# Delta rule per pair of heads: the next pair's triangular inputs, the products on the old state, and the wait for the state stores

## The chip, the cores and the metric

The kernel runs on one core of one Trainium2 chip. The metric is the device time of one execution in microseconds, the median of several runs. The engines of the core are TensorE (PE in the profile, with its weight loads as PEld), VectorE (DVE), ScalarE (ACT), GpSimd (POOL) and SyncE (SP), which here only issues transfers and waits.

## What is computed

One inference step of two decoder layers for a prompt group (1 sequence of 512 tokens) and a sample group (8 sequences of 8 tokens, each with a state from before). The change touches only the gated delta rule of the second layer: 8 heads of width 128, in chunks. Cut to what matters:

```python
def gated_delta(q, k, v, g, beta, s0, chunk):
    gc = jnp.cumsum(rs(g), axis=2)
    kb, vb = k * beta[..., None], v * beta[..., None]
    decay = exp(where(incl, gc_i - gc_j, -inf))
    amat = where(strict, (kb @ k.T) * decay, 0)
    tmat = triangular_solve(amat + eye, eye)          # lower, unit diagonal
    u = tmat @ vb
    w = tmat @ (kb * exp(gc))
    qk = where(incl, (q @ k.T) * decay, 0)
    qg = q * exp(gc)
    kdec = k * exp(gc_last - gc)
    def step(s, inp):                                  # over the chunks
        v_new = u_c - w_c @ s
        o = qg_c @ s + qk_c @ v_new
        s = s * exp(gc_last) + kdec_c.T @ v_new
        return s, o
```

The kernel takes chunks of 128 tokens for the prompt (4 tiles) and puts the 64 sample tokens into a fifth tile. The states after the last chunk are outputs: one of 128x128 per head for the prompt, eight per head for the samples.

## The kernel before

All matrices are fp32. `gdn` works in two halves of 4 heads. A half is a row of stages: `project_conv` (input projection and convolution), `gdn_l2norm`, two calls of `gdn_pair` with two heads each, then `gdn_norm`, which starts the output. A stage (`stage`, L90) gives each engine one program. It ends when every engine's program has ended: semaphores are cleared and all engines meet at a barrier, so nothing of the next stage starts before. Two stages are thus joined by whatever engine ends last, SP included.

Within `gdn_pair` each engine has its instructions in a fixed order, first for head a = 0, then for head a = 1, and waits on counters of the others (`PE[...]`, `AC[...]`, `DV[...]`, `PO[...]` name the steps). A tile called `[P, 640]` holds the five tiles of one head. The parts of a pair are:

- **Opening.** POOL builds two inputs per head, `UG` (upper triangle times the gate, L2810) and `IB` (identity times beta, L2811). PE sums each over the partitions with a matrix of ones (`R`, `BR`, L2921 and L2922). DVE and ACT make the decay matrix from `R` (L2867, L2868, L2828) and multiply it with `BR` and with k.k (L2872, L2875) to give `LT`, and with k.q to give `QKD` (L2878). DVE then masks `LT` (L2880), subtracts it from the identity to give the first `TT` (L2881), and makes `kbg`, `kdec` (L2884, L2885) from the turned k and `vb` (L2887) from the turned v, which lie in PSUM; the last of these is the step "tok". PE turns `TT` after "tok" (L2931).
- **Inverse.** Six rounds, k = 1 to 6. POOL masks `LT` for the round (`AL`, L2818), PE makes three products (L2926), ACT and DVE take them out of PSUM (L2838, L2893, L2896).
- **Chunks.** Four steps over the prompt's tiles with the state `S` of 128x128 (L2977 to L2988, L2904).
- **Samples' part.** PE multiplies the eight old states `S0` with `w` ("svn", L2993 and L2995), ACT copies, PE turns ("svt", L3000), ACT copies again into `VN4` (L2854). Then PE makes the output with `qg` and the same eight `S0` ("so", L3004 and L3006), while DVE spreads `VN4` over eight blocks (`VNm`, L2908). PE makes the update ("ss", L3012, two matmuls of 512 columns per head), and DVE scales `S0` (L2912, after "so") and adds the update (L2915).

SP loads the `S0` of both heads at the stage's start (L2797), stores `S` when the chunks are done (L2800) and `S0` at the end (L2803), and then waits until all these stores have landed (L2805). The page and the timeline count an fp32 matmul as two records, so a product of one 128x128 weight matrix is x2.

Of the kernel before, what the change touches and what calls it, by code (L numbers as in the profile page):

```python
# [2542 lines left out]
def gdn(nc, K):  # L2543

    with ExitStack() as ctx:
# [11 lines left out]
        for p in range(2):  # L2557
            with ExitStack() as c2:
                SX = c2.enter_context(nc.sbuf_tensor(f"g_SX{p}", [P, 3 * HH, TP], F32))
                cols = gdn_cols(p)  # L2560
                with ExitStack() as c3:
                    keep = c3.enter_context(nc.sbuf_tensor(f"g_keep{p}", [P, 12, 27], F32))
                    project_conv(nc, K, f"gconv{p}", K.at["gconv"] + 6 * p, 12, HW[:, p], False, SX, keep, high)
                    gdn_l2norm(nc, K, SX, high, 2 * HH, HH, (keep, rows, cols))
                for q in range(HH // 2):
                    gdn_pair(nc, K, C, SX, high, (2 * q, 2 * q + 1), HH * p)
                gdn_norm(nc, K, C, SX, high, HH, HH * p)
# [95 lines left out]
def norm_over_partitions(nc, K, tiles, high, scale, apply, conv=None):  # L2663
# [4 lines left out]
    with stage(nc, "squared", "summed", "logged", "rs_ready", "used", "kept_turned", "kept_out") as (  # L2668
            block, squared, summed, logged, rs_ready, used, kept_turned, kept_out):
        if conv:  # L2670
# [3 lines left out]
            def _(sp):  # L2674
                sp.wait_ge(kept_out, 3)
                store_conv_state(K, sp, rows, K.o_gdn_conv_p[0], K.o_gdn_conv_s[0], cols)

# [60 lines left out]
def gdn_pair(nc, K, C, SX, high, heads, h_base):  # L2738
# [5 lines left out]
    with ExitStack() as ctx:  # L2744
        def sb(name, shape):
            return ctx.enter_context(nc.sbuf_tensor(f"{name}_{h_base + heads[0]}", shape, F32))

        B = []
        for a in range(2):
            b = Ctx()  # L2750
            if a == 0:
                big = high[:, 0:8 * TP].rearrange("p (s n) -> p s n", s=8)
            else:
                big = sb("k_big", [P, 8, TP])[:]
            tiles = [big[:, i, :] for i in range(8)]
            b.XS, b.AL, b.TM, b.E, b.DT, b.LT, b.QKD, b.TT = tiles
            b.VNm = big[0:TS, 0:2, :].rearrange("p s n -> p (s n)")[:, 0:NB * P].rearrange("p (b n) -> p b n", b=NB)
            b.VN4 = big[0:TS, 0:2, :].rearrange("p s n -> p (s n)")[:, NB * P:(NB + 1) * P]
            b.kbg = K.X[:, 3584 + TP * a:3584 + TP * (a + 1)]
            b.S = sb(f"k_S{a}", [P, P])[:]  # L2760
            b.S0 = K.X[:, 1536 + D * a:1536 + D * (a + 1)].rearrange("p (b n) -> p b n", b=NB)
            h = heads[a]
            b.q, b.k, b.v = SX[:, h, :], SX[:, 4 + h, :], SX[:, 8 + h, :]
            b.kdec, b.vb, b.w, b.qg, b.O = b.k, b.v, b.LT, b.DT, b.q
            b.h = h_base + h
            b.bank = 4 * a
            b.A = K.PSF[:, 2048 * a:2048 * a + TP]
            b.Bp = K.PSF[:, 2048 * a + 1024:2048 * a + 1024 + TP]
            B.append(b)

        def t5(ap):
            return ap.rearrange("p (t n) -> p t n", n=P)

        def tile_(ap, t):
            return ap[:, t * P:(t + 1) * P]


        KS = range(1, LEVELS)
        pe_steps = (["R", "BR", "kk", "qk", "ktok", "vtok", "turnT"]
                    + [x for k in KS for x in ([("X", k), ("TX", k), ("TXT", k)] if k < LEVELS - 1 else [("X", k), ("TXT", k)])]  # L2780
                    + ["w"] + [x for t in range(NT) for x in (("vn", t), ("s", t))] + ["svn", "svt", "so", "ss"])
        act_steps = (["E", "DT", "TM"] + [("XS", k) for k in KS] + ["w"] + [("VN", t) for t in range(NT)]
                     + ["VT", "VN4", "O"])
        dve_steps = (["DT", "LT1", "LT", "QKD", "TT0", "tok"]
                     + [x for k in KS for x in ([("TM", k), ("TT", k)] if k < LEVELS - 1 else [("TT", k)])]
                     + [("S", t) for t in range(NT)] + ["VNm", "S0"])
        pool_steps = ["UG", "IB"] + [("AL", k) for k in KS] + ["qg"]
        at = [{s: i + 1 for i, s in enumerate(steps)} for steps in (pe_steps, act_steps, dve_steps, pool_steps)]
        PE, AC, DV, PO = at
        with stage(nc, "pe_0", "pe_1", "act_0", "act_1", "dve_0", "dve_1", "pool_0", "pool_1", "s0_in", "dve_link") as (  # L2790
                block, pe0, pe1, act0, act1, dve0, dve1, pool0, pool1, s0_in, dve_link):
            pes, acts, dves, pools = (pe0, pe1), (act0, act1), (dve0, dve1), (pool0, pool1)

            @block.sync
            def _(sp):
                for b in B:
                    sp.dma_start(b.S0, K.state_gdn[0, :, b.h].rearrange("b k v -> k b v")).then_inc(s0_in, 16)  # L2797
                for a, b in enumerate(B):
                    sp.wait_ge(dves[a], DV[("S", NT - 1)])
                    sp.dma_start(K.o_gdn_p[0, 0, b.h], b.S).then_inc(K.state_out, 16)  # L2800
                for a, b in enumerate(B):
                    sp.wait_ge(dves[a], DV["S0"])
                    sp.dma_start(K.o_gdn_s[0, :, b.h].rearrange("b k v -> k b v"), b.S0).then_inc(K.state_out, 16)  # L2803
                K.n_state_out += 4
                sp.wait_ge(K.state_out, 16 * K.n_state_out)  # L2805

            @block.gpsimd
            def _(pool):
                for a, b in enumerate(B):
                    pool.tensor_tensor(t5(b.XS), K.U5, bc(C.g[:, :, b.h], 2, P), ALU.mult).then_inc(pools[a], 1)  # L2810
                    pool.tensor_tensor(t5(b.TM), bc(K.ident[:], 1, TT), bc(C.beta[:, :, b.h], 2, P),  # L2811
                                       ALU.mult).then_inc(pools[a], 1)
                for k in KS:
                    for a, b in enumerate(B):
                        pool.wait_ge(dves[a], DV["LT"])
                        if k > 1:
                            pool.wait_ge(pes[a], PE[("X", k - 1)])
                        pool.tensor_tensor(t5(b.AL), t5(b.LT), bc(K.LV[:, k, :], 1, TT), ALU.mult).then_inc(pools[a], 1)  # L2818
                for a, b in enumerate(B):
                    pool.wait_ge(dves[a], DV["QKD"])  # L2820
                    pool.tensor_tensor(b.qg, b.q, b.E, ALU.mult).then_inc(pools[a], 1)

            @block.scalar
            def _(act):
                for a, b in enumerate(B):
                    act.wait_ge(dves[a], DV["DT"])
                    act.activation(b.E, b.A, ACT.Exp).then_inc(acts[a], 1)
                    act.activation(b.DT, b.DT, ACT.Exp).then_inc(acts[a], 1)  # L2828
                for a, b in enumerate(B):
                    act.wait_ge(pes[a], PE["turnT"])  # L2830
                    act.copy(b.TM, b.A).then_inc(acts[a], 1)
                for k in KS:
                    for a, b in enumerate(B):
                        n = TP if k < 3 else SEQ
                        act.wait_ge(pes[a], PE[("X", k)])
                        if k > 1:
# [807 lines left out]
```

## Time and profile before

| | |
|---|---|
| median of 3 runs | 3188.43 us (3186.65 to 3192.07) |
| profiled execution | 3190.75 us, its span 3189.0 us |
| PE busy | 2721.1 us (85%) |
| DVE busy | 1291.4 us (40%) |
| ACT busy | 914.4 us (29%) |
| POOL busy | 888.4 us (28%) |
| mean granted TensorE clock | 0.899 of 2.4 GHz |

The median is of runs without a profile; the profiled execution is a run of its own. Its span goes from the first to the last instruction, and 1.75 us lie around it. The shares are means over stages with different limits, so they say little about a stage of 100 us; for that the timeline is needed, which lists instructions in order of time with what ended the idle time before them.

### The profile page before, as it was taken

The numbers are of one execution on the slowest core, as the hardware profiler recorded it, in microseconds if no ns is written. First come the engines' busy times: TensorE is split into PE (matmuls) and PEld (weight loads), VectorE is DVE, ScalarE is ACT, GpSimd is POOL, SyncE is SP. The second block draws the span as 40 slices with busy tenths as digits, with TensorE's granted clock in tenths as the row PEclk, the third lists the DMA queues.
The fourth block names the chain that finished last, engine by engine and source line by source line (L and its number), as shares of the span: only waits on it lengthen the run. The fifth ranks groups of instructions, "written<-read, shape, count | busy, mean of one in ns | idle before, by whom it ended". The sixth has DMA issues, their size and how long they took to land. (4 is left out here: it accounts for less than half of the span.)

```text
span 3189.0 us, 47332 instructions
## 1 busy us (share of the span) xinstructions
PE 2721.1 (85%) x19759; PEld 2444.5 (77%) x19759; DVE 1291.4 (40%) x2573; ACT 914.4 (29%) x1589; POOL 888.4 (28%) x443
## 2 busy tenths in 40 slices
PE   6766579989798999977968976897999888799998
PEld 5634279855697999977957875886998668799997
DVE  5665331177614222242643455344011643422224
ACT  4211032056424211243331133122222543521122
POOL 2131022023234333333322222231322003533331
PEclk9866789899799999988888888797999999899998
DMA  4100226454031222222111011001223072122221
GB/s 151 57 1 27 66 76 107 123 167 195 1 80 54 80 81 92 80 66 88 55 41 29 4 54 54 16 15 45 85 92 101 8 199 88 56 80 81 93 80 57
DMA packets 217827, 232.94 MB, mean 73 GB/s; under 512 B 41036, under 2 KB 186924, under 8 KB 217006
## 3 DMA queue, kind: packets, MB, share of 16 engines
q1 hardware_dynamic: 207086, 225.47, 23.2%
q10 hardware_dynamic: 10528, 4.44, 0.5%
q8 instruction: 157, 2.57, 0.3%
q14 instruction: 56, 0.46, 0.0%
HBM read 207.93 MB, written 48.35 MB: 80 GB/s over the span
## 5 line engine op out<-in xcount | busy, mean ns | idle before, releaser
L271 POOL TENSOR_TENSOR WRr<-WR,WH 128x2048 fp32r<-128x2048 f32 (+3 forms) x98 | 443.1, 4521 | 840.5 <-ACT WH L259 840.5
L2099 PE MATMUL PS<-HHr,WRr 128*128 128x288 f32 x1152 | 343.3, 298 | 0.0
L411 PE MATMUL PS<-HHr,WH 128*128 128x288 f32 (+1 forms) x928 | 277.5, 299 | 49.5 <-PEq L97 49.5
L411 PE MATMUL PS<-YTr,WRr 128*128 128x288 f32 x1024 | 304.0, 297 | 0.0
L259 ACT CAST WH<-WR 128x2048 fp32r<-128x2048 f32 (+3 forms) x98 | 180.5, 1842 | 362.2 <-DMA WR<-in_mlp_w 189.4
L411 PE MATMUL PS<-YTr,lt_WX 128*128 128x288 f32 x1408 | 281.8, 295 | 0.0
L411 PE MATMUL PS<-HTr,WH 128*128 128x288 f32 (+1 forms) x928 | 277.1, 299 | 0.0
L411 PE MATMUL PS<-HHr,WRr 128*128 128x288 f32 (+1 forms) x928 | 277.0, 298 | 0.0
L411 PE MATMUL PS<-WH,HHr 128*128 128x256 f32 (+3 forms) x760 | 220.0, 289 | 21.2 <-PEq L97 21.2
L2099 PE MATMUL PS<-HHr,WH 128*128 128x288 f32 x768 | 228.6, 298 | 9.4 <-POOL HTr L2087 8.7
L271 POOL TENSOR_TENSOR WRr<-WR,lt_WX 128x2048 fp32r<-128x2048 f32 x35 | 162.1, 4632 | 234.1 <-ACT lt_WX L259 234.1
L411 PEld LDWEIGHTS PS<-YTr,lt_WX 128*128 128x128 f32 x1408 | 227.1, 188 | 0.1
L2099 PE MATMUL PS<-HTr,WH 128*128 128x288 f32 x768 | 226.9, 295 | 0.0
L2099 PEld LDWEIGHTS PS<-HHr,WRr 128*128 128x128 f32 x1152 | 219.5, 191 | 0.0
L411 PE MATMUL PS<-WRr,HHr 128*128 128x256 f32 (+3 forms) x760 | 217.0, 286 | 0.0
L411 PE MATMUL PS<-WH,HTr 128*128 128x256 f32 (+3 forms) x760 | 217.0, 286 | 0.0
L411 PEld LDWEIGHTS PS<-HHr,WH 128*128 128x128 f32 (+1 forms) x928 | 174.4, 188 | 52.5 <-issue 51.0
L411 PEld LDWEIGHTS PS<-YTr,WRr 128*128 128x128 f32 x1024 | 192.8, 188 | 0.0
L411 PEld LDWEIGHTS PS<-HHr,WRr 128*128 128x128 f32 (+1 forms) x928 | 174.2, 188 | 1.5
L411 PEld LDWEIGHTS PS<-HTr,WH 128*128 128x128 f32 (+1 forms) x928 | 174.2, 188 | 1.5
L2483 DVE TENSOR_TENSOR YT<-YT 128x576 f32<-128x576 f32 x64 | 55.0, 860 | 276.9 <-ACT YT L2372 266.3
L2498 DVE TENSOR_TENSOR lt_AHf<-lt_AHf,PS 128x576 f32<-128x576 f32 x96 | 72.5, 755 | 210.0 <-PE PS L411 210.0
(646 smaller groups left out, 6215.5 us busy)
## 6 DMA issues: line engine op xcount, KB each, us to landing
WR<-in_mlp_w SPq DMA_DIRECT2D x64, 1024.0 KB, 5.3
WR<-in_cd_w_in SPq DMA_DIRECT2D x34, 1024.0 KB, 5.5
out_dil_s<-in_cache_dil_kv SPq DMA_DIRECT2D x2, 7936.0 KB
WR<-in_ab_w_in SPq DMA_DIRECT2D x10, 1024.0 KB, 5.4
past_rows<-in_cache_nsa_kv SPq DMA_DIRECT2D x16, 256.0 KB, 3.5
YT<-in_state_ssm ACTq DMA_DIRECT2D x16, 256.0 KB, 4.6
out_ssm_s<-YT SPq DMA_DIRECT2D x16, 256.0 KB
WR<-in_ab_w_in SPq DMA_DIRECT2D x16, 256.0 KB, 4.3
```

What stands on the lines that cost most here:

```text
L259: act.copy(high_slot(K, i, used), K.WR[:, n % RING, 0:used]).then_inc(K.hi, 1)
L271: pool.tensor_tensor(K.WRr[:, n % RING, 0:used], K.WR[:, n % RING, 0:used], high_slot(K, i, used).bitcast(F32), ALU.subtract).then_inc(K.l ...
L411: last = pe.matmul(out, a, b, start=(n == 0), stop=(n == 3 * len(terms) - 1))
L2099: last = pe.matmul(out, a[:, k, c], h[:, k, x], start=(n == 0), stop=(n == 3 * KT - 1))
L2483: dve.tensor_tensor(x, x, x, ALU.mult).then_inc(sq_done, 1)
L2498: dve.tensor_tensor(acc, acc, ps, ALU.add).then_inc(acc_done, 1)
```

## The change

`gdn_pair` is called twice per half, as before, now with the number of the pair (0 or 1), with buffers that both calls share, and with one `S` tile for the four heads of the half. Its parts are changed as follows.

- **Inputs.** `UG` now lies in the tile `TT` and `IB` in `LT`, in place of `XS` and `TM`. Pair 0 builds `UG` on POOL and `IB` on DVE at its start. In its samples' part, after "svn", POOL builds both for pair 1, and pair 1 starts with them.
- **Opening.** The first mask of `LT` goes from DVE to POOL, in front of the masks of the rounds. `vb` goes from DVE to ACT, as five products of 128x128. "tok" comes after `kdec`.
- **Samples' part.** One matmul per old state takes 16 columns (8 of `qg` and 8 of `w`, neighbours in one buffer) in place of two with 8 columns. "so" is then one product with `VN4`. The turned rows go to another PSUM bank. DVE scales `S0` after "svn".
- **Stores.** SP no longer waits for the stores at the end of the stage. Pair 1 waits for them before it loads `S0`, and SP waits in `gdn_norm`.

```diff
+        else:                                  # norm_over_partitions, in gdn_norm
+            @block.sync
+            def _(sp):
+                sp.wait_ge(K.state_out, 16 * K.n_state_out)
...
+            b.UG, b.IB = b.TT, b.LT
...
             @block.sync
             def _(sp):
+                if pair:
+                    sp.wait_ge(K.state_out, 16 * K.n_state_out)
                 for b in B:
                     sp.dma_start(b.S0, K.state_gdn[0, :, b.h].rearrange("b k v -> k b v")).then_inc(s0_in, 16)
...
-                sp.wait_ge(K.state_out, 16 * K.n_state_out)
...
             @block.gpsimd
             def _(pool):
-                for a, b in enumerate(B):
-                    pool.tensor_tensor(t5(b.XS), K.U5, bc(C.g[:, :, b.h], 2, P), ALU.mult).then_inc(pools[a], 1)
-                    pool.tensor_tensor(t5(b.TM), bc(K.ident[:], 1, TT), bc(C.beta[:, :, b.h], 2, P),
-                                       ALU.mult).then_inc(pools[a], 1)
+                if pair == 0:
+                    for a, b in enumerate(B):
+                        pool.tensor_tensor(t5(b.UG), K.U5, bc(C.g[:, :, b.h], 2, P), ALU.mult).then_inc(pools[a], 1)
+                for a, b in enumerate(B):
+                    pool.wait_ge(dves[a], DV["LT"])
+                    pool.tensor_tensor(t5(b.TT), t5(b.LT), bc(K.LV[:, 0, :], 1, TT), ALU.mult).then_inc(pools[a], 1)
...
+                if not last_pair:
+                    for a, b in enumerate(B):
+                        pool.wait_ge(pes[a], PE["svn"])
+                        pool.tensor_tensor(t5(b.UG), K.U5, bc(C.g[:, :, b.h + 2], 2, P), ALU.mult)
+                        pool.tensor_tensor(t5(b.IB), bc(K.ident[:], 1, TT), bc(C.beta[:, :, b.h + 2], 2, P), ALU.mult)
...
             def _(act):
+                for a, b in enumerate(B):
+                    act.wait_ge(pes[a], PE["vtok"])
+                    for t in range(TT):
+                        last = act.mul(tile_(b.vb, t), tile_(b.Bp, t), C.beta[:, t, b.h:b.h + 1])
+                    last.then_inc(acts[a], 1)
...
             def _(dve):
+                if pair == 0:
+                    for a, b in enumerate(B):
+                        dve.tensor_tensor(t5(b.IB), bc(K.ident[:], 1, TT), bc(C.beta[:, :, b.h], 2, P), ALU.mult).then_inc(dves[a], 1)
...
-                    do(dve.tensor_tensor(t5(b.TT), t5(b.LT), bc(K.LV[:, 0, :], 1, TT), ALU.mult))
+                    dve.wait_ge(pools[a], PO["L0"])
                     dve.tensor_tensor(t5(b.TT), bc(K.ident[:], 1, TT), t5(b.TT), ALU.subtract).then_inc(dves[a], 1)
...
-                    dve.tensor_tensor(t5(b.kdec), t5(b.A), bc(C.dl[:, :, b.h], 2, P), ALU.mult)
-                    dve.wait_ge(pes[a], PE["vtok"])
-                    dve.tensor_tensor(t5(b.vb), t5(b.Bp), bc(C.beta[:, :, b.h], 2, P), ALU.mult).then_inc(dves[a], 1)
+                    dve.tensor_tensor(t5(b.kdec), t5(b.A), bc(C.dl[:, :, b.h], 2, P), ALU.mult).then_inc(dves[a], 1)
...
-                    dve.wait_ge(pes[a], PE["so"])
+                    dve.wait_ge(pes[a], PE["svn"])
                     do(dve.tensor_tensor(b.S0, b.S0, bc(b.E[:, SEQ + NS - 1:TOK:NS], 2, P), ALU.mult))
...
             def _(pe):
-                    out = K.PS[:, b.bank + 3, 0:TS]
-                    pe.matmul(out, b.vb[0:TS, SEQ:TP], b.TT[0:TS, SEQ:TOK], start=True, stop=False, skip_group_check=True)
-                    for s in range(NB):
-                        last = pe.matmul(out[:, s * NS:(s + 1) * NS], b.S0[:, s, :], b.w[:, SEQ + s * NS:SEQ + (s + 1) * NS],
-                                         start=False, stop=(s == NB - 1), skip_group_check=True)
-                    last.then_inc(pes[a], 1)
+                    out = K.PS[:, b.bank + 3, 256:256 + 2 * TS].rearrange("p (i n) -> p i n", i=2)
+                    for r in range(NB):
+                        c = slice(r * NS, (r + 1) * NS)
+                        pe.matmul(out[:, :, c], b.S0[:, r, :], b.big[:, 4:6, SEQ + r * NS:SEQ + (r + 1) * NS],
+                                  start=(r == 0), stop=False, skip_group_check=True)
+                    pe.matmul(out[:, 1, :], b.vb[0:TS, SEQ:TP], b.TT[0:TS, SEQ:TOK], start=False, stop=True,
+                              skip_group_check=True).then_inc(pes[a], 1)
...
-                    out = K.PS[:, b.bank + 3, 256:256 + TS]
-                    pe.matmul(out, b.VN4, b.QKD[0:TS, SEQ:TOK], start=True, stop=False, skip_group_check=True)
-                    for s in range(NB):
-                        last = pe.matmul(out[:, s * NS:(s + 1) * NS], b.S0[:, s, :], b.qg[:, SEQ + s * NS:SEQ + (s + 1) * NS],
-                                         start=False, stop=(s == NB - 1), skip_group_check=True)
-                    last.then_inc(pes[a], 1)
+                    pe.matmul(K.PS[:, b.bank + 3, 256:256 + TS], b.VN4, b.QKD[0:TS, SEQ:TOK], start=False, stop=True,
+                              skip_group_check=True).then_inc(pes[a], 1)
```

## Rows read from the trace of the kernel before

**Rows 1.** Stages: window, its us, busy us (instructions) per engine, PEclk, DMA share, GB/s.
```profile
1639.60:1740.20 100.60, 86.54 (x556) 75.22 (x556) 41.77 (x56) 17.28 (x36) 26.34 (x18) 0.81 0.08 23
...
1712.40:1740.20 27.80, 22.31 (x84) 16.59 (x82) 7.59 (x7) 2.35 (x8) 0.00 (x0) 0.55 0.15 43
```

**Rows 2.** Timeline at the ends of first and last pair: start, us, engine, line, tiles.
```profile
1734.80 1.22 DVE L2915 TENSOR_TENSOR X<-X,PS 128x1024 f32<-128x1024 f32 x1 [2.12 <-PE PS L3012]
...
1732.70 3.73 SPq L2803 DMA_DIRECT2D out_gdn_s<-X  x2
...
1740.20 1.26 POOL L2810 TENSOR_TENSOR YT<-UN,g_g 128x640 f32<-128x640 f32 x1 [42.72 <-POOLq L97]
...
2163.20 1.22 DVE L2915 TENSOR_TENSOR X<-X,PS 128x1024 f32<-128x1024 f32 x1 [2.12 <-PE PS L3012]
...
2169.02 2.40 ACT L2694 ACTIVATE YT<-g_SX 128x576 f32<-128x576 f32 x4 [12.25 <-PEq L97]
```

**Rows 3.** Timeline where a stage ends without a store (gdn_l2norm, then pair 0).
```profile
1633.40 5.44 DVE L2717 SCALAR_TENSOR_TENSOR g_SX<-g_SX,YT 128x576 f32<-128x576 f32 x8 [17.60 <-ACT YT L2701]
...
1639.65 1.26 POOL L2810 TENSOR_TENSOR YT<-UN,g_g 128x640 f32<-128x640 f32 x1 [38.45 <-POOLq L97]
```

**Rows 4.** Timeline of PE in the samples' part, first pair; last row: fourth pair.
```profile
1712.83 1.95 PE L2995 MATMUL PS<-YT,X 128*128 128x8 f32 x16
...
1715.07 3.58 PE L2995 MATMUL PS<-k_big,X 128*128 128x8 f32 x16
...
1719.93 3.58 PE L3006 MATMUL PS<-YT,X 128*128 128x8 f32 x16
...
1727.57 3.78 PE L3012 MATMUL PS<-YT,g_SX 64*128 64x512 f32 x4
...
2155.97 3.78 PE L3012 MATMUL PS<-YT,g_SX 64*128 64x512 f32 x4
```

**Rows 5.** Timeline of PE in the inverse of the first pair, products of 128 columns.
```profile
1663.09 2.34 PE L2926 MATMUL PS<-YT 128*128 128x128 f32 x10
...
1675.28 1.28 PE L2926 MATMUL PS<-k_big 128*128 128x128 f32 x10
```

**Rows 6.** Timeline of DVE in the samples' part of the first pair.
```profile
1719.24 1.22 DVE L2908 TENSOR_TENSOR YT<-YT,SELT 64x1024 f32<-64x1024 f32 x1 [6.31 <-ACT YT L2854]
...
1731.45 1.22 DVE L2915 TENSOR_TENSOR X<-X,PS 128x1024 f32<-128x1024 f32 x1 [2.48 <-PE PS L3012]
```

**Rows 7.** Timeline of POOL, DVE, PE and ACT in the opening of the first pair.
```profile
1652.33 1.55 POOL L2818 TENSOR_TENSOR k_big<-k_big,LV 128x640 f32<-128x640 f32 x1
...
1652.40 0.82 DVE L2878 TENSOR_TENSOR YT<-PS,YT 128x640 f32<-128x640 f32 x1
...
1654.26 0.81 DVE L2880 TENSOR_TENSOR YT<-YT,LV 128x640 f32<-128x640 f32 x1
...
1661.10 0.81 DVE L2887 TENSOR_TENSOR g_SX<-PS,g_beta 128x640 f32<-128x640 f32 x1
...
1653.31 2.35 PE L2931 MATMUL PS<-ident,g_SX 128*128 128x128 f32 x20
1659.78 0.77 PE L2931 MATMUL PS<-ident,YT 128*128 128x128 f32 x5 [4.12 <-DVE g_SX L2887]
1661.97 1.33 PE L2931 MATMUL PS<-ident,k_big 128*128 128x128 f32 x5 [1.43 <-DVE g_SX L2887]
...
1660.58 0.69 ACT L2831 COPY YT<-PS 128x640 f32<-128x640 f32 x1 [10.15 <-PE PS L2931]
```

**Rows 8.** Timeline where POOL and DVE both read two SBUF tiles (two places).
```profile
253.62 3.38 POOL L1058 TENSOR_TENSOR YT<-UN,s_la 128x512 f32<-128x512 f32 x2 [20.84 <-PE PS L1030]
...
254.16 1.95 DVE L1094 TENSOR_TENSOR d_xdw<-d_xx,s_dlast 128x1024 f32<-128x1024 f32 x1
...
1595.98 5.22 POOL L271 TENSOR_TENSOR WRr<-WR,WH 128x2048 fp32r<-128x2048 f32 x1 [7.50 <-ACT WH L259]
...
1596.66 4.63 DVE L828 SCALAR_TENSOR_TENSOR YT<-YT,g_HW 128x64 f32<-128x64 f32 x1
```

**Rows 9.** Timeline of PE at the start of the second pair.
```profile
1741.52 2.07 PE L2921 MATMUL PS<-YT,ones 128*128 128x512 f32 x2 [6.77 <-POOL YT L2810]
```

## What the change does to the time, predicted before it ran

> **What bounds the kernel now.** The granted clock of the whole run says nothing on this change, so I read by stage: first the windows, to see what one pair costs, then the timeline of each engine in it. The four pairs last 98 to 101 us each (the first is in [rows 1]) and go through the same steps, so I work out the first and say where another differs. PE is busy for 87 of the first 100.6 us, DVE for 42 and POOL for 26 [rows 1], so PE is the engine to relieve, but only where it is the last thing waited for. The samples' part, 27.8 of the 100.6 us, has a granted clock of 0.55 [rows 1]: most of it runs at 1.2 GHz. All engines meet at a barrier at each stage's end, so a microsecond taken from the last engine of a pair is taken from the kernel, and nothing running across the barrier can eat it.
>
> **The stage's end.** DVE ends the first pair's last addition at 1736.02 (1734.80 plus 1.22), and the next stage begins at 1740.20: 4.2 us in which no engine computes. After the fourth pair it is 2164.42 to 2169.02, 4.6 us [rows 2]; the two between have 4.2. Where a stage ends with no store, DVE ends at 1638.84 and the next begins at 1639.65, 0.8 us [rows 3]. The difference of 3.4 (once 3.8) is the store. Not all of it goes: SP must still issue the second store after DVE's end. The two issues span 3.73 us from 1732.70, so the last is through at 1736.43 [rows 2], 0.4 us after DVE. I take 3.0, 3.0, 3.0 and 3.4, in all 12.4 us; the bounds are 8 (if the issue ends only some 1.5 us after DVE) and 14 (all but the 0.8). Where the waits go: the one in pair 1 has only SP's loads of `S0` behind it, which PE needs some 70 us later; the one in the norm lies in a stage of 19 us, and the stores need 4. The Trainium skill (DMA: Bandwidth & Descriptors, Anatomy of one DMA) gives about 2.0 us as the fixed cost of a transfer; by it alone this term would be an estimated 8 us. The rows' 3.4 includes moving the bytes, and they decide.
>
> **The samples' part.** Sixteen records with 8 columns (8 old states of one head) take 1.95 us at 2.4 GHz and 3.58 us at 1.2 GHz [rows 4], that is 0.12 and 0.22 each. Ten records with 128 columns take 1.28 and 2.34 us [rows 5], 0.13 and 0.23 each. Sixteen times the columns cost no more: what is paid is the weight load, and 16 columns in place of 8 cost nothing. (Bounds: 0 to 0.1 us per head, from the same rows.) So "svn" stays as it is and "so" shrinks to one product. Where does the end of the chain go? Now "so" begins at 1719.3 and "ss" at 1727.57 [rows 4]. `VNm` of head 0, which "ss" needs, starts at 1719.24 and takes 1.22 [rows 6]: it is done at 1720.5. With "so" gone "ss" waits for it and begins at 1720.6, 7.0 us earlier; it takes its 3.6 us per head either way, and DVE's last addition follows 0.1 us after it [rows 2, 4]. DVE has by then done both `VNm` and both scalings (four of 1.22, to 1723.9), before the first "ss" product at 1724.2, so it is not late. In the fourth pair the clock fell some 3 us later and "so" was cheaper: "ss" began at 2155.97 [rows 4] and would begin at 2149.6, so 6.4 us. Sum without POOL: 7.0, 7.0, 7.0, 6.4.
>
> **POOL beside DVE.** This is what speaks against the change, and it needs care. A DVE operation that takes one input from PSUM runs at full speed beside POOL: 0.82 us, started 0.07 us after a POOL mask [rows 7]. One with both inputs in SBUF doesn't. The 128x64 operation at 1596.66 took 4.63 us and ended 0.1 us after POOL's operation had ended; that POOL operation took 5.22 us where the same takes 4.5 alone, having waited for DVE first [rows 8]. At 253.62 two POOL operations of 1.04 us span 3.38 us and DVE's of 1.22 takes 1.95 in between [rows 8]: they take turns, one whole operation each. The Trainium skill (SBUF — State Buffer, Who interferes with whom) states the same: a VectorE instruction with two SBUF inputs and a GpSimd one that reads SBUF hold shared reads against each other for a whole instruction. By that rule, the trace agrees.
>
> In pair 0 POOL builds `UG` and `IB` (1.26 each [rows 2]) for head 0 from 1714.8 to 1717.4 and for head 1 from 1718.6, beside `VNm` and the scalings, all with two SBUF inputs. `VNm` of head 0 waits for the first `UG` until 1719.9 and ends at 1721.1; "ss" follows, 0.6 us later than above. The rest alternates and is through before "ss" ends. Cost: 0.6 in each of two pairs (bounds 0 and 2.0, if POOL keeps its turn for both operations). Term for the samples' part: 27.4 less 1.2, or 26.2 us.
>
> **The opening.** At first sight it gains much. DVE loses four operations there, `vb` twice and the mask twice; "tok" of head 1 now comes at 1661.91 (1661.10 plus 0.81), and PE turns `TT` at 1661.97 [rows 7]. DVE comes to this work at 1654.3, as now, and has one subtraction and two products per head left: 6 at a pace of 0.74 (the pace of the ten that now fill 1654.3 to 1661.9), "tok" at 1658.8, so 3.1 us earlier. But the subtraction has both inputs in SBUF and now stands beside POOL's masks. POOL has `LT` of head 1 at 1652.3 [rows 7] and goes on without a pause: mask of head 0 (in the place of `AL` now, until 1652.3), of head 1 (to 1653.9), `AL` of head 0 to 1655.4, `AL` of head 1. DVE's first subtraction, ready at 1654.3, waits until 1655.4 and ends at 1656.1; POOL's next takes until 1657.5; the second subtraction ends at 1658.2; four products of 0.74 end at 1661.1. "tok" is 0.8 us earlier, not 3.1. I take 0.7 per pair, 2.8 us (bounds 0 and 3.1 per pair). `vb` on ACT costs nothing: ACT is idle for 10.15 us there and takes 0.69 us for 640 columns in one piece [rows 7]; five pieces per head can't take more than 3.5 us each head, and both heads fit. The idle time of PE before the turn stays near the 4.12 us [rows 7] after which its clock falls, so I leave the clock alone: the turn of head 1 still takes 1.33 us and the first inverse products 2.34 [rows 5, 7].
>
> **The inputs.** Pair 1 no longer waits for POOL: PE began at 1741.52 [rows 9], 1.3 us after the stage began, which goes twice: 2.7 us. In pair 0 POOL still builds `UG`, now beside DVE's `IB`, both reading SBUF: if DVE comes first, `UG` is 0.8 us late. I take 0.4 twice, so minus 0.8 (bounds 0 and minus 1.6). The other builds of POOL had lain beside PE's sums and bring nothing.
>
> **Sum.** 12.4 + 26.2 + 2.8 + 2.7 - 0.8 = 43.3 us. The profiled execution took 3190.75 us, 2.3 above the median of 3188.43; 43.3 less is 3147.4 of the one and 3145.1 of the other. I forecast 3145.
>
> **The rivals.**
> *No turns in the opening* (the subtraction runs at full speed beside the masks, or POOL is ready before): "tok" is 3.1 us earlier. The idle time of PE before the turn shrinks from 4.1 to about 1.7 us and the clock may then stay at 2.4 GHz, so that 25 records go at 0.13 in place of 0.23 us. That is 2.4 to 4.5 us more per pair, 10 to 18 in all: 3127 to 3135. For it speaks only that no row shows these very two operations side by side. Chance 0.12.
> *The clock holds through the samples' part.* In the fourth pair it fell 3 us later than in the first. With a shorter part it might not fall before "ss" ends, which would take 1.9 in place of 3.6 us per head: 3 to 5 us per pair, for some pairs; 3127 to 3138. Against it: 7 us of "ss" at 1.2 GHz never raised it [rows 4], and "svn" with small products comes first as now. Chance 0.10.
> *The store's wait stays in another dress.* If the 4.2 us are the barrier after a stage with DMAs, and not the landing, the change doesn't do what it says there: 12.4 us less gain, 3157. Rows 3 speak against it, though there no DMA was under way. Chance 0.12.
> *A pair that runs cold: slower than before.* The clock now rises 4 to 6 us into each pair. Were the earlier stretch so changed that it stays at 1.2 GHz through opening, inverse and chunks, then the 470 records outside the samples' part (556 less 84 [rows 1]) would cost 0.10 us more each: 47, less the 7 that are cold already, 40 us per pair. It decides from the second cold pair on: 3225. Against it: the first inverse products ran at 1.2 GHz and those 12 us later at 2.4 [rows 5], after an idle time that stays the same. Chance 0.04.
> *The forecast as summed*: 0.62, with its own range of 3137 to 3153 from the bounds.
>
> **The numbers.** The range reaches to 3128, into the two faster cases, and to 3158, past the case of the store; what is left out is the cold case and the far edge of the faster ones. A measurement of this kernel tells about 0.2% (6 us) from no change. All cases but the cold one, and what I can't name, are faster by more: faster 0.93, same 0.03, slower 0.04.
>
> **What would show it.** Between the last L2915 of a pair and the next stage's first instruction there should be 1.2 us. "ss" should start about 0.1 us after the first `VNm`, and `VNm` in pair 0 should take 1.9 us where it takes 1.22 in pair 1. The subtraction in the opening should take 1.8 us for head 0 and 2.2 for head 1 in place of 0.82. The joint products should take 1.95 or 3.6 us for 16 records. The second pair's PE should begin with the stage. I am wrong if the subtraction takes 0.82 us, if the gap at the end stays at 4 us, or if 16 columns cost more than 8. The pairs should last 91, 88, 91 and 86 us.

## The result and the profile after

| | before | after |
|---|---|---|
| median | 3189.62 us of 4 runs (3186.65 to 3192.07) | 3144.99 us of 4 runs (3137.14 to 3145.88) |
| ratio, with its 95% interval | | 0.9856 (0.9841 to 0.987) |
| profiled execution | 3190.75 us | 3145.86 us, its span 3144.1 us |
| mean granted TensorE clock | 0.899 | 0.907 |
| the four pairs together | 398.1 us | 350.8 us |

The four windows of the pairs, and the samples' part of the first (from the first "svn" product to the next stage). Columns: window, its us, then busy us and instructions of PE, PEld, DVE, ACT and POOL, granted clock, DMA share, GB/s.

```profile
1640.40:1728.35 87.95, 76.37 (x525) 65.35 (x525) 46.44 (x54) 19.88 (x46) 33.87 (x22) 0.87 0.08 23
1728.35:1813.16 84.81, 75.92 (x524) 65.06 (x524) 40.83 (x52) 19.88 (x47) 24.90 (x16) 0.88 0.10 27
1944.44:2034.39 89.95, 78.97 (x524) 67.93 (x525) 46.14 (x54) 19.87 (x46) 33.94 (x22) 0.84 0.08 21
2034.39:2122.51 88.12, 79.01 (x524) 67.89 (x524) 40.83 (x52) 19.87 (x46) 24.96 (x16) 0.85 0.09 26
1711.07:1728.35 17.28, 13.36 (x53) 7.90 (x51) 9.41 (x7) 2.25 (x8) 5.91 (x4) 0.64 0.18 51
```

Against [rows 1]: the first pair went from 100.60 to 87.95 us, with 31 PE records fewer and a clock of 0.87 where it was 0.81. DVE is busy for 4.7 us more in it than before, although it has fewer operations to do (54 for 56): some of them now take longer. To see where the time went, each pair is cut at three points that can be read in both timelines: the start of the last turn of `TT`, the first "svn" product, and the end of the last addition of the update to `S0`. Us, before and after, for pairs 1 to 4 in order of time (pairs 1 and 3 are the ones with `pair` = 0 in the code):

| stretch | before | after | gain |
|---|---|---|---|
| opening: stage's start to last turn | 22.3, 21.6, 22.1, 21.5 | 21.5, 19.5, 21.4, 20.1 | 5.0 |
| inverse and chunks: to "svn" | 50.5, 50.1, 50.4, 50.1 | 49.2, 48.9, 50.7, 50.8 | 1.5 |
| samples' part: to the last addition's end | 23.6, 23.8, 23.6, 21.4 | 15.6, 14.9, 16.5, 15.9 | 29.6 |
| gap: to the next stage's first instruction | 4.18, 4.17, 4.18, 4.60 | 1.70, 1.57, 1.38, 1.35 | 11.1 |

The gains add up to 47.3 us. The profiled executions differ by 44.9, so 2.4 us were lost outside the pairs, in code that the change doesn't touch: the first pair begins 0.75 us later (1640.40 for 1639.65), the rest comes after it.

The opening of the first pair in the timeline after (start, us, engine, line, operation, tiles, and idle time before with what ended it):

```profile
1651.51 1.55 POOL L2818 TENSOR_TENSOR YT<-YT,LV 128x640 f32<-128x640 f32 x1 [8.04 <-DVE YT L2894]
...
1653.09 1.54 POOL L2818 TENSOR_TENSOR k_big<-k_big,LV 128x640 f32<-128x640 f32 x1
...
1654.59 1.55 POOL L2824 TENSOR_TENSOR YT<-YT,LV 128x640 f32<-128x640 f32 x1
1655.02 1.81 DVE L2900 TENSOR_TENSOR YT<-ident,YT 128x640 f32<-128x640 f32 x1
1655.37 2.69 ACT L2843 ACTIVATE g_SX<-PS,g_beta 128x128 f32<-128x128 f32 x10 [4.17 <-PE PS L2947]
1656.11 2.12 POOL L2824 TENSOR_TENSOR k_big<-k_big,LV 128x640 f32<-128x640 f32 x1
1656.75 2.15 DVE L2900 TENSOR_TENSOR k_big<-ident,k_big 128x640 f32<-128x640 f32 x1
...
1661.89 1.33 PE L2947 MATMUL PS<-ident,k_big 128*128 128x128 f32 x5 [0.69 <-DVE g_SX L2904]
```

The subtraction (L2900) takes 1.81 and 2.15 us in place of the 0.82 that such an operation takes alone. Its first ends at 1656.83, that is 0.69 us after POOL's mask of the same time (1654.59 to 1656.14): about the 0.74 at which DVE operations of this size follow each other at full speed (its products here start 0.73 apart), so it began only when POOL was through. The second ends 0.67 us after POOL's second mask. That mask itself takes 2.12 in place of 1.55 us, since it had to let the first subtraction by. They take turns, as forecast.

The samples' part of the same pair:

```profile
1711.07 1.86 PE L3013 MATMUL PS<-YT,X 128*128 128x16 f32 x16
...
1713.21 1.96 PE L3013 MATMUL PS<-k_big,X 128*128 128x16 f32 x16
...
1713.37 1.26 POOL L2831 TENSOR_TENSOR YT<-UN,g_g 128x640 f32<-128x640 f32 x1 [17.20 <-PE PS L3015]
1714.59 1.26 POOL L2832 TENSOR_TENSOR YT<-ident,g_beta 128x640 f32<-128x640 f32 x1
...
1715.81 1.26 POOL L2831 TENSOR_TENSOR k_big<-UN,g_g 128x640 f32<-128x640 f32 x1
...
1716.10 2.05 DVE L2925 TENSOR_TENSOR YT<-YT,SELT 64x1024 f32<-64x1024 f32 x1 [4.48 <-ACT YT L2870]
...
1718.20 3.78 PE L3028 MATMUL PS<-YT,g_SX 64*128 64x512 f32 x4 [0.90 <-DVE YT L2925]
...
1725.43 1.22 DVE L2931 TENSOR_TENSOR X<-X,PS 128x1024 f32<-128x1024 f32 x1 [1.43 <-PE PS L3028]
...
1728.35 2.05 PE L2937 MATMUL PS<-YT,ones 128*128 128x512 f32 x2 [2.95 <-PEq L97]
```

From top to bottom: sixteen records with 16 columns take 1.86 us, no more than the 1.95 of those with 8 [rows 4]. "svn" of head 1 takes 1.96, where it took 3.58 [rows 4]: it now runs before the clock has fallen. POOL builds the next pair's inputs, and `VNm` (L2925), which fell on POOL's third operation, takes 2.05 us for 1.22. "ss" (L3028) follows it and still runs at 1.2 GHz. The next stage's first product comes 1.70 us after the last addition's end (1726.65), and it is PE's: it waits for no input of POOL.

### The profile page after: what moved, and what is told of

It reads as the page before. It is cut to its first block and busy times, and to the rows that moved or that the text cites. A ratio compares the mean times of both kernels' runs of the same rounds, so it can differ in the third digit from the quotient of the medians.

```text
span 3144.1 us, 47114 instructions
## 1 busy us (share of the span) xinstructions
PE 2689.2 (86%) x19631; PEld 2414.0 (77%) x19631; DVE 1297.9 (41%) x2561; ACT 924.6 (29%) x1629; POOL 900.1 (29%) x447
## 3 DMA queue, kind: packets, MB, share of 16 engines
q1 hardware_dynamic: 207086, 225.47, 23.6%
## 5 line engine op out<-in xcount | busy, mean ns | idle before, releaser
L411 PE MATMUL PS<-HHr,WH 128*128 128x288 f32 (+1 forms) x928 | 277.7, 299 | 49.5 <-PEq L97 49.5
```

The costliest lines, as they stand in the source:

```text
L411: last = pe.matmul(out, a, b, start=(n == 0), stop=(n == 3 * len(terms) - 1))
```

## The experiments

Each kernel is the changed one with one edit, timed against the kernel before in the same job. The kernel before had a median of 3189.52 us beside e1 to e4 and of 3188.87 beside the others. "Pairs" below is the sum of the four pairs' lengths in the profiled execution (350.8 after the change); medians of two versions closer than some 7 us are not told apart, since the four runs of the changed kernel alone spread over 8.7 us, and those of e3 over 10.2.

### e1: the stores awaited at the end of each pair again

```diff
-            if pair:
-                sp.wait_ge(K.state_out, 16 * K.n_state_out)
...
             K.n_state_out += 4
+            sp.wait_ge(K.state_out, 16 * K.n_state_out)
```

> The changed kernel with SP waiting for all stores at each pair's end again, all else as changed. My theory (the landing of the stores was what the barrier waited for): the time from the last addition of a pair to the next stage, 1.35 to 1.70 us in the changed kernel, goes back to 4.2 to 4.6 us, 11 us over the four pairs: 3156 us. Rival (the barrier costs that much after any stage with transfers, and the gain came otherwise): the gap stays near 1.5 us and the time at 3145.

Measured: 3154.35 us (3151.34 to 3157.05), ratio 0.9888 (0.9872 to 0.9905). The gaps are 4.52, 4.37, 4.20 and 4.16 us, 11.25 more than after, and the medians differ by 9.4. In the timeline of e1, the last addition of the first pair and the first product of the second:

```profile
1729.16 1.22 DVE L2930 TENSOR_TENSOR X<-X,PS 128x1024 f32<-128x1024 f32 x1 [1.43 <-PE PS L3027]
...
1734.90 2.05 PE L2936 MATMUL PS<-YT,ones 128*128 128x512 f32 x2 [5.78 <-PEq L97]
```

4.52 us lie between the end of the one (1730.38) and the start of the other, where they were 1.70 with the wait moved. So what filled the gap was the landing of the stores, not the barrier, and the rival of "another dress" is out: the same transfers are in flight across the barrier after the change, and it costs 1.4 to 1.7 us.

### e2: the products on the old state made separately again

```diff
-                dve.wait_ge(pes[a], PE["svn"])
+                dve.wait_ge(pes[a], PE["so"])
...
-                    pe.matmul(out[:, :, c], b.S0[:, r, :], b.big[:, 4:6, SEQ + r * NS:SEQ + (r + 1) * NS],
+                    pe.matmul(out[:, c], b.S0[:, r, :], b.w[:, SEQ + r * NS:SEQ + (r + 1) * NS],
...
-                pe.matmul(K.PS[:, b.bank + 3, 256:256 + TS], b.VN4, b.QKD[0:TS, SEQ:TOK], start=False, stop=True,
-                          skip_group_check=True).then_inc(pes[a], 1)
...
+                pe.matmul(out, b.VN4, b.QKD[0:TS, SEQ:TOK], start=True, stop=False, skip_group_check=True)
+                for r in range(NB):
+                    last = pe.matmul(out[:, r * NS:(r + 1) * NS], b.S0[:, r, :], b.qg[:, SEQ + r * NS:SEQ + (r + 1) * NS],
+                                     start=False, stop=(r == NB - 1), skip_group_check=True)
```

The scaling of `S0` goes back behind "so" with them, since "so" again reads the unscaled states.

> The changed kernel with two matmuls of 8 columns per old state again (the product with w in svn, that with qg in so), and the scaling of the old state after so; all else as changed. Theory (the weight load is paid, the columns are not): so takes 3.6 us per head again at 1.2 GHz (1.9 at 2.4), svn keeps its length, ss starts 6 to 7.5 us later: 24 to 30 us over four pairs, 3169 to 3175. Rival (16 columns cost more than 8, so that part of the gain was paid back in svn): svn gets shorter here by over 0.3 us per head, and the time ends below 3168.

Measured: 3172.4 us (3169.13 to 3173.46), ratio 0.9949 (0.9932 to 0.9966), so 27.4 above the changed kernel. From the first "svn" to the first "ss" it took 15.00, 13.37, 14.45 and 13.31 us, where after it takes 7.13, 6.40, 8.01 and 7.44: 27.15 in all, near the difference of the medians. In the timeline of e2, first pair:

```profile
1711.80 1.85 PE L3013 MATMUL PS<-YT,X 128*128 128x8 f32 x16
...
1719.17 3.58 PE L3026 MATMUL PS<-YT,X 128*128 128x8 f32 x16
...
1726.80 2.92 PE L3032 MATMUL PS<-YT,g_SX 64*128 64x512 f32 x3
```

Eight columns take 1.85 us for 16 records where 16 columns took 1.86: joining the products is free, and what it saves is the whole second pass (L3026).

### e3: the mask of round 0 back on VectorE

```diff
-            for a, b in enumerate(B):
-                pool.wait_ge(dves[a], DV["LT"])
-                pool.tensor_tensor(t5(b.TT), t5(b.LT), bc(K.LV[:, 0, :], 1, TT), ALU.mult).then_inc(pools[a], 1)
...
-                dve.wait_ge(pools[a], PO["L0"])
+                do(dve.tensor_tensor(t5(b.TT), t5(b.LT), bc(K.LV[:, 0, :], 1, TT), ALU.mult))
```

> The changed kernel with the first mask of LT on DVE again, in front of each subtraction; vb stays on ACT. Theory (DVE and POOL take turns when both read two SBUF tiles): POOL's round-1 masks are over before DVE masks and subtracts, the subtraction takes 0.82 us in place of 1.81 and 2.15, DVE's last product ends 1.3 us EARLIER although DVE does two operations more; 1.3 us per pair, 5 us in all, 3140, a little more if the clock stays up. Rival (the mask's move to POOL was worth its two operations of 0.82 on DVE): the last product ends 1.6 us later per pair, 3151.

Measured: 3138.86 us (3130.8 to 3141.03), ratio 0.9845 (0.9829 to 0.9861). In the timeline of e3, opening of the first pair:

```profile
1648.36 1.55 POOL L2821 TENSOR_TENSOR k_big<-k_big,LV 128x640 f32<-128x640 f32 x1
...
1650.28 0.81 DVE L2896 TENSOR_TENSOR YT<-YT,LV 128x640 f32<-128x640 f32 x1
1651.13 0.83 DVE L2897 TENSOR_TENSOR YT<-ident,YT 128x640 f32<-128x640 f32 x1
```

POOL's masks are over (1649.91) before DVE comes to its mask (L2896) and its subtraction (L2897), and both run at full speed. The openings are 19.6, 18.9, 20.8 and 19.2 us, 4.1 us shorter in all than after, though DVE has two operations more. So moving the mask to POOL brought nothing: DVE paid more for the turns (1.0 + 1.3 us per pair) than the mask had cost it (two at a pace of 0.75). By the medians e3 is 6.1 us below the changed kernel, which is not told apart: the runs of both overlap. By the pairs it is 9.0 us shorter: 4.1 in the openings, and 2.8 in inverse and chunks and 2.1 in the samples' part, where nothing was edited and more products ran at 2.4 GHz.

### e4: POOL's masks of round 1 held until the subtractions are done

```diff
             for k in KS:
                 for a, b in enumerate(B):
                     pool.wait_ge(dves[a], DV["LT"])
+                    if k == 1:
+                        pool.wait_ge(dves[1], DV["TT0"])
```

> The changed kernel with one wait more: POOL begins the masks of round 1 only when DVE has done both subtractions. Theory (turns): both subtractions take 0.82 us, the last product of DVE in the opening ends near 3.1 us less late than at 1661.9 of before, that is 2.3 us before that of the changed kernel; the round-1 masks end before PE needs them. 2.3 us per pair, 9 us in all: 3136; and where PE's shorter idle time keeps it at 2.4 GHz, 1 to 2 us more per pair, down to 3128. Rival (the subtraction is slow for another reason): subtractions stay at 1.8 and 2.2 us, PE waits for the later masks instead, and the time is 3145 to 3151.

Measured: 3123.85 us (3121.02 to 3125.97), ratio 0.9793 (0.9777 to 0.981): one wait more, and 21 us less than the changed kernel. In the timeline of e4, opening of the second pair:

```profile
1739.46 0.82 DVE L2902 TENSOR_TENSOR YT<-ident,YT 128x640 f32<-128x640 f32 x1
...
1740.19 0.82 DVE L2902 TENSOR_TENSOR k_big<-ident,k_big 128x640 f32<-128x640 f32 x1
1741.16 1.54 POOL L2826 TENSOR_TENSOR YT<-YT,LV 128x640 f32<-128x640 f32 x1 [2.08 <-DVE k_big L2902]
```

The subtractions take 0.82 us each, and POOL's mask begins after them. The openings are 17.9, 17.5, 19.1 and 17.4 us: 10.6 us less than after. That is 2.65 us per pair; the prediction had put the turns at 2.4 (3.1 without them, 0.7 with them). But inverse and chunks also became shorter, though nothing in them was edited: 49.5, 47.9, 47.9 and 47.9 us, together 6.5 less. The fourth pair shows why. After the change:

```profile
2053.03 0.77 PE L2947 MATMUL PS<-ident,YT 128*128 128x128 f32 x5 [4.01 <-DVE g_SX L2904]
2054.49 1.33 PE L2947 MATMUL PS<-ident,k_big 128*128 128x128 f32 x5 [0.70 <-DVE g_SX L2904]
2055.61 2.34 PE L2942 MATMUL PS<-YT 128*128 128x128 f32 x10
```

and in e4:

```profile
2039.63 0.77 PE L2949 MATMUL PS<-ident,YT 128*128 128x128 f32 x5 [1.67 <-DVE g_SX L2906]
2041.09 0.77 PE L2949 MATMUL PS<-ident,k_big 128*128 128x128 f32 x5 [0.69 <-DVE g_SX L2906]
2041.69 1.28 PE L2944 MATMUL PS<-YT 128*128 128x128 f32 x10
```

PE idles for 4.01 us before the turn after the change, and its next products run at 1.2 GHz (2.34 us for ten). In e4 it idles for 1.67 us and they run at 2.4 GHz (1.28). In pairs 2 to 4 of e4 the clock doesn't fall there at all; in pair 1 it still does.

The other runs fit a link between this idle time and the clock, but for that one pair. Where PE idled for 4.0 us before the turn (16 pairs, of the changed kernel, e1, e2 and e5) or for 3.4 (the four of e3), the turn of head 1 took 1.33 us, all at 1.2 GHz. Where it idled for 1.67 us (e4, e6) or 0.94 (e7), it took 0.77 in 11 pairs of 12; in pair 1 of e4 it took 0.99, with the same 1.67 us of idle time as pair 1 of e6, whose clock held. So the idle time isn't all that decides; what else does wasn't tested.

This is the first rival of the prediction, made to happen by a wait: its forecast was 3127 to 3135. The measured 3124 lies under that, and under the 3128 to 3136 expected of e4; most of the difference is a samples' part 2.1 us shorter over the four pairs, where "svn" of head 1 ran at 2.4 GHz in all of them.

### e5: the inputs built at the stage's start in every pair

The tests of the pair's number before `IB` on DVE and before PE's two waits go in the same way.

```diff
-            if pair == 0:
-                for a, b in enumerate(B):
-                    pool.tensor_tensor(t5(b.UG), K.U5, bc(C.g[:, :, b.h], 2, P), ALU.mult).then_inc(pools[a], 1)
+            for a, b in enumerate(B):
+                pool.tensor_tensor(t5(b.UG), K.U5, bc(C.g[:, :, b.h], 2, P), ALU.mult).then_inc(pools[a], 1)
...
-            if not last_pair:
-                for a, b in enumerate(B):
-                    pool.wait_ge(pes[a], PE["svn"])
-                    pool.tensor_tensor(t5(b.UG), K.U5, bc(C.g[:, :, b.h + 2], 2, P), ALU.mult)
-                    pool.tensor_tensor(t5(b.IB), bc(K.ident[:], 1, TT), bc(C.beta[:, :, b.h + 2], 2, P), ALU.mult)
```

> The changed kernel with UG (POOL) and IB (DVE) built at the start of both pairs, and nothing built for the next pair in the samples' part. Theory: the second pair of a half starts PE 1.3 us later than its stage, twice, minus 2.6 us; the first pair's VNm goes from 2.05 and 2.28 to 1.22 us and ss starts 0.6 to 0.8 us earlier, twice, plus 1.4 us. Net 1 us slower, 3146 us, within noise; the trace decides. Rival (building ahead costs nothing): VNm stays at 2 us for another reason, and the whole 2.6 us are lost.

Measured: 3140.74 us (3137.97 to 3143.69), ratio 0.9851 (0.9835 to 0.9867), 4.3 below the changed kernel's median, which is not told apart. Both halves of the trade are in the trace. In the timeline of e5, start of the second pair:

```profile
1726.83 1.26 POOL L2814 TENSOR_TENSOR YT<-UN,g_g 128x640 f32<-128x640 f32 x1 [31.01 <-POOLq L97]
...
1728.14 2.08 PE L2931 MATMUL PS<-YT,ones 128*128 128x512 f32 x2 [3.94 <-POOL YT L2814]
```

PE begins 1.3 us after the stage does, and the openings of pairs 2 and 4 are 20.8 and 21.0 us where after they are 19.5 and 20.1, so 1.2 and 0.9 us longer. In return `VNm` takes 1.22 us in every pair, and from "svn" to "ss" it takes 6.30 us in pair 1 and 7.48 in pair 3, for 7.13 and 8.01. Building ahead saves 2.2 us in the openings and costs 1.4 before "ss": where the inputs are built matters next to nothing. (Pair 3 stays above 6.30 because "svn" of head 1 took 2.76 us there, partly at 1.2 GHz, as it does after.)

### e6: both orders, POOL kept off VectorE twice

```diff
+                    if k == 1:
+                        pool.wait_ge(dves[1], DV["TT0"])
...
                 for a, b in enumerate(B):
                     pool.wait_ge(pes[a], PE["svn"])
+                    if a:
+                        pool.wait_ge(dves[1], DV["VNm"])
```

> The kernel with round 1 of POOL's masks after the subtractions (3123.85 us), with one wait more: POOL builds head 1's inputs for the next pair only after both VNm. Theory (turns): VNm of the first pairs takes 1.22 us again, ss starts 0.6 to 0.8 us earlier in two pairs; the builds stand beside the scalings instead, which have time. 1.4 us less, 3122; no change that a median can tell, so the trace decides. Rival: the builds beside the scalings delay the last additions, ends of the first pairs come later, 3125.

Measured: 3120.81 us (3120.04 to 3123.85), ratio 0.979 (0.9776 to 0.9804). This is the lowest median of all, though e4's is not told apart from it. In the timeline of e6, samples' part of the first pair:

```profile
1713.20 1.22 DVE L2929 TENSOR_TENSOR YT<-YT,SELT 64x1024 f32<-64x1024 f32 x1 [4.48 <-ACT YT L2874]
...
1715.70 2.12 POOL L2835 TENSOR_TENSOR k_big<-UN,g_g 128x640 f32<-128x640 f32 x1 [2.74 <-DVE k_big L2929]
1716.72 2.17 DVE L2932 TENSOR_TENSOR X<-X,k_big 128x1024 f32<-128x1024 f32 x1
...
1718.93 1.22 DVE L2935 TENSOR_TENSOR X<-X,PS 128x1024 f32<-128x1024 f32 x1
1721.70 1.22 DVE L2935 TENSOR_TENSOR X<-X,PS 128x1024 f32<-128x1024 f32 x1 [1.55 <-PE PS L3032]
```

`VNm` (L2929) takes 1.22 us in all pairs, and "ss" begins 6.3 us after "svn" in all four, where in e4 it was 7.14 in pairs 1 and 3. The turns haven't gone, they have moved: a scaling of `S0` (L2932) now takes 2.17 us. The first addition (L2935) begins right behind it, 4.46 us after "ss" where it is 3.88 in pair 2. But the last addition still idles for 1.55 us before it, waiting for "ss" of head 1, and the samples' part is as long as in pair 2 (14.74 us), so the longer scaling costs nothing. The same builds of POOL thus cost 0.8 us when they fall on `VNm` and nothing when they fall on the scaling.

### e7: `kbg` on ScalarE in place of `vb`

On top of e6:

```diff
-                dve.wait_ge(pes[a], PE["ktok"])
-                dve.tensor_tensor(t5(b.kbg), t5(b.A), bc(C.beg[:, :, b.h], 2, P), ALU.mult)
+                dve.wait_ge(acts[a], AC["kbg"])
...
-                    last = act.mul(tile_(b.vb, t), tile_(b.Bp, t), C.beta[:, t, b.h:b.h + 1])
+                    last = act.mul(tile_(b.kbg, t), tile_(b.A, t), C.beg[:, t, b.h:b.h + 1])
...
+            for a, b in enumerate(B):
+                dve.wait_ge(pes[a], PE["vtok"])
+                dve.tensor_tensor(t5(b.vb), t5(b.Bp), bc(C.beta[:, :, b.h], 2, P), ALU.mult).then_inc(dves[a], 1)
```

> e6 with the product kbg on ACT (in five pieces per head, from the turned k) and vb back on DVE, after tok. Theory (DVE's chain up to tok sets the turn of TT): two DVE products of 0.73 leave that chain, tok of head 1 comes 1.4 us earlier, 5.5 us over four pairs, 3117; vb on DVE lies in DVE's idle time before round 1. Rival (ACT's pieces are now the last thing waited for, as kdec must wait for them, both reading one PSUM bank): tok comes less than 0.5 us earlier and the time stays at 3122.

Measured: 3122.43 us (3121.5 to 3125.8), ratio 0.9794 (0.9781 to 0.9808): the same as e6. The openings did become shorter, 16.4 to 18.0 us where e6 has 17.6 to 19.1 in pairs 2 to 4 (1.1 to 1.3 us each) and 2.4 us in the first. It isn't more because ScalarE is now just in time: DVE waits for it. In the timeline of e7, second pair:

```profile
1740.33 0.82 DVE L2907 TENSOR_TENSOR g_SX<-PS,g_dl 128x640 f32<-128x640 f32 x1 [0.24 <-ACT X L2847]
```

The gain didn't reach the median. In its profiled execution the first pair began 2.4 us later than that of e6 (1643.56 for 1641.18), in code that is the same in both, and in pairs 3 and 4 the way from "svn" to "ss" took 7.86 and 8.01 us for 6.30, since the clock fell before it. The pairs sum to 327.7 us for 330.2. Whether the earlier fall of the clock follows from the shorter opening or is chance stays open.

## Why the prediction was right, point by point

The forecast of 3145 us is the median to within 0.1 us, and the change is faster, as forecast. That it came so close is partly luck: the steps summed to 43.3 us, the pairs gave 47.3, and 2.4 were lost outside them; the rest is how medians and profiled executions lie to each other. The median of the kernel before also came out 1.2 us higher (3189.62) than the 3188.43 from which the 43.3 were taken.

**The stage's end**, 12.4 forecast, 11.1 measured (e1: 11.25). The mechanism was right: the landing of the store filled the gap. The term was a tenth too large, since I left 1.2 us (0.4 for SP's issue after the last addition, 0.8 from there to the next stage), and 1.35 to 1.70 us stayed. The 0.4 was right:

```profile
1724.03 3.04 SPq L2808 DMA_DIRECT2D out_gdn_s<-X  x2
```

The issues are through at 1727.07, 0.42 us after the last addition (1726.65), as in the other pairs. What was too small is the 0.8, taken from a stage that ends without a store [rows 3]: it was 1.28 us here and 0.94 in the fourth pair. Why wasn't tested. The prediction set the Trainium skill's fixed cost of about 2.0 us (DMA: Bandwidth & Descriptors, Anatomy of one DMA) against this term, 8 us by that alone. The section gives it for transfers that GpSimd issues, and adds the bytes over 436 GB/s; by the whole of it a store of 512 KB takes an estimated 3.2 us, 12.8 over four pairs. The trace agrees roughly: 2.5 to 3.25 us per pair were gained, and e1 gave back 2.8 in each.

**The samples' part**, 26.2 forecast, 29.6 measured. This is the mis-sized term. That 16 columns cost the same as 8 held to 0.01 us (1.86 and 1.85 in e2). That `VNm` becomes the last thing "ss" waits for held, and its 1.9 us in pairs 1 and 3 came as 2.05 and 1.74. What I had wrong is the sentence that "svn" stays as it is. Its products for head 1 took 3.58, 3.58, 3.58 and 1.95 us before and 1.96, 1.96, 2.76 and 2.72 after, 3.3 us less in all, which is nearly the whole difference of 3.4. In pairs 1 and 2 the clock fell later: in the first it had been down 2.2 us after the first product on an old state had begun [rows 4]; now it was still up 4.1 us after it (1711.07 to 1715.17). Why wasn't tested, but it isn't the joining: e2, with 8 columns again, has 3.29, 1.95, 2.74 and 1.95. "ss" itself stayed cold, so the rival by which the clock holds to the end didn't come.

**The opening**, 2.8 and 2.7 less 0.8 forecast, 4.7 in all; 5.0 measured. The two durations on which it rested, 1.8 and 2.2 us for the subtraction, were 1.81 and 2.15. They were worked out from two places elsewhere in the kernel [rows 8], where other tiles of other sizes took turns, and the rule carried over. The Trainium skill says the same (SBUF — State Buffer, Who interferes with whom): a VectorE instruction with two SBUF inputs and a GpSimd instruction that reads SBUF shut each other out for a whole instruction; here the trace agrees, with 0.82 us alone (e4) and 2.15 beside POOL. One small step was wrong: I took 0.8 us off for `IB` on DVE standing in the way of `UG`. In both pairs that build there (1 and 3) POOL came first and took its 1.26 us as before [rows 2], as the timeline after shows, and DVE's `IB` waited, which nothing needed yet:

```profile
1640.40 1.26 POOL L2815 TENSOR_TENSOR YT<-UN,g_g 128x640 f32<-128x640 f32 x1 [38.51 <-POOLq L97]
1640.41 1.93 DVE L2883 TENSOR_TENSOR YT<-ident,g_beta 128x640 f32<-128x640 f32 x1 [0.83 <-PEq L97]
```

**Not forecast:** inverse and chunks gained 1.3 us in each of the first two pairs and lost 0.3 to 0.7 in the others, by where the clock rose; the forecast had left the clock alone there. The 1.5 us in all are no more than kernels differ by that have the same code there: 199.6 us over the four pairs after, 200.0 in e1, 197.7 in e5.

**The pairs' lengths**, forecast as 91, 88, 91 and 86 us, were 87.95, 84.81, 89.95 and 88.12. Three were shorter by 1 to 3 us and the fourth longer by 2: its "svn" of head 1 took 2.72 us, partly cold, its inverse and chunks 0.7 us more than before, and its opening gained 0.6 us less than forecast. Two small slips of the working hardly count: by its own step "ss" of the fourth pair would begin at 2149.3 and not 2149.6 (`VNm` is done at 2149.22 there), and the ten operations from 1654.3 to 1661.9 go at a pace of 0.76, not 0.74.

**The rivals.** The store in another dress was ruled out by e1. No turns in the opening didn't happen in the changed kernel, and e4 shows what it would have been worth: 3124 us, under the 3127 that ended that case. That the clock holds to the end of "ss" didn't happen in any pair. The cold pair didn't come in any run. That the turns could be taken away by one wait, and that the change as it stands leaves 21 to 24 us lying there (e4, e6), I hadn't seen; the prediction had the price of it in its first rival, as a thing that would happen or not, not as a thing to arrange.

## What to carry to other kernels

Work handed from VectorE to GpSimd wasn't free here where VectorE had both inputs in SBUF at that time (0.82 us became 1.81 and 2.15), and was free where one of them lay in PSUM (0.82 us beside a mask [rows 7]). List for each GpSimd operation what VectorE does beside it, and let it fall on one that nobody waits for, if need be by a wait more. Where TensorE pauses in the middle of a stage, ask how long: shortening a pause from 4.0 to 1.7 us gave back the pause and, in most pairs, the time that the products behind it had spent at 1.2 GHz. An fp32 product with 8, 16 or 128 columns took the same 0.12 to 0.13 us a record here at 2.4 GHz [rows 4, 5], so two products of few columns with the same weights are better made as one, and a wait for a store belongs where its buffer is next written, not where the stage ends.

## What was not expected of the hardware

- An added wait made the kernel 21 us faster (e4), 19.2 of them in the pairs: 10.6 us from the turns, 6.5 us from inverse and chunks at the higher clock, 2.1 from the samples' part.
- Between two queued operations of GpSimd a waiting one of VectorE is let in, and the other way round. The subtraction ended 0.69 and 0.67 us after the mask it had waited for, and the second mask took 2.12 in place of 1.55 us. So VectorE's loss is what is left of GpSimd's operation, not all that GpSimd has queued.
- In the same unchanged code ahead of the pairs the profiled executions, one of each kernel, scatter: the first pair began between 1636.94 us (e3) and 1643.56 us (e7). That is more than most single steps of this study are worth, and the reason why each was read inside the pairs and not from the medians alone. One execution of each doesn't tell whether the kernels differ there or only their executions.
